# The gMLP gate of a two-layer decoder step: weights and biases prepared within the projection of v, v normalised by ScalarE in eight groups, one evacuation per block

## The reference, cut to what matters

```python
z = gelu(h @ w_in); u, v = split(z, 2)            # 3072 columns each
v = layer_norm(v, ln_g, ln_b)
ws = where(tril, w_s, 0)                          # 8 groups of 128x128
s = einsum('gts,bnsgc->bntgc', ws, vp) + b_s      # per chunk of 128 tokens, 384 columns per group
return (u * s) @ w_out, v                         # for the sample tokens v is an output too
```

## Time and profile before

| | |
|---|---|
| median of three runs | 2092.73 us (2079.18 to 2095.14) |
| profiled execution | 2092.21 us |
| its span, first to last instruction | 2090.40 us |
| TensorE matmul busy | 1862.7 us (89%) |
| VectorE busy | 1060.9 us (51%) |
| ScalarE busy | 540.6 us (26%) |
| GpSimd busy | 301.7 us (14%) |
| mean granted clock of TensorE | 0.933 |

### The profile page before, as it was taken

How to read it: one execution, slowest core, us unless ns; L and a number is a source line. 1 busy time by engine, 2 the same in 40 slices (tenths; PEclk the granted TensorE clock), 3 DMA queues, 4 the chain that set the end, 5 groups by cost and what they waited for, 6 DMA issues and landing times.

```text
span 2090.4 us, 35666 instructions
## 1 busy us (share of the span) xinstructions
PE 1862.7 (89%) x14217; PEld 1697.8 (81%) x14217; DVE 1060.9 (51%) x1400; ACT 540.6 (26%) x822; POOL 301.7 (14%) x263
## 2 busy tenths in 40 slices
PE   5866788687678879999999999969999999999998
PEld 4765555455455479999999999969999999999997
DVE  2599998987885345432333333274323353323321
ACT  4321232212222033321232233312313332212221
POOL 1220000000000001420241100022403223202300
PEclk8987898789899789999999999989999999999999
DMA  6247776899998722332323322211322323332321
GB/s 211 82 125 244 240 242 188 261 311 309 300 305 261 245 73 82 91 101 92 91 86 96 96 79 74 66 34 41 103 93 89 101 81 95 98 92 81 101 91 62
DMA packets 218302, 288.04 MB, mean 138 GB/s; under 512 B 12993, under 2 KB 149778, under 8 KB 217890
## 3 DMA queue, kind: packets, MB, share of 16 engines
q1 hardware_dynamic: 215306, 281.95, 42.3%
q0 software_dynamic: 656, 1.51, 0.5%
q10 hardware_dynamic: 2208, 2.75, 0.4%
HBM read 274.96 MB, written 11.21 MB: 137 GB/s over the span
## 4 chain that ended last, share of the span: by engine, by line
PE 70%; DVE 18%; SPq 3%; DMA 3%; issue 3%; ACT 2%; ACTq 0%; DVEq 0%
PE ps L1604 17%; PE ps L1606 17%; PE ps L1605 17%; PE ps L1425 4%; DVE kbuf L1109 4%; PE ps L1427 4%; PE ps L1426 4%; DVE Sc L1112 4%; DMA vbuf<-in_cache_v 2%; SPq L499 2%; SPq L498 1%; PE ps L1460 1%; DVE w_lo L488 1%; PE ps L1671 1%; PE ps L1393 1%
## 5 line engine op out<-in xcount | busy, mean ns | idle before, releaser
L488 DVE TENSOR_TENSOR w_lo<-raw,w_hi 128x1024 fp32r<-128x1024 f32 x238 | 328.0, 1386 | 486.9 <-ACT w_hi L481 485.6
L1604 PE MATMUL ps<-xg_hi,w_hi 128*128 128x260 f32 x1408 | 398.9, 283 | 0.5 <-DVE sTs L1380 0.5
L1606 PE MATMUL ps<-xg_hi,w_lo 128*128 128x260 f32 x1408 | 398.6, 283 | 0.0
L1605 PE MATMUL ps<-xg_lo,w_hi 128*128 128x260 f32 x1408 | 397.4, 282 | 0.0
L1425 PE MATMUL ps<-w_hi,xg_hi 128*128 128x256 f32 (+1 forms) x1200 | 366.1, 305 | 20.9 <-DVE w_lo L488 6.0
L481 ACT ACTIVATE w_hi<-raw 128x1024 fp32r<-128x1024 f32 x248 | 258.7, 1052 | 459.0 <-PE ps L1606 397.0
L1426 PE MATMUL ps<-w_lo,xg_hi 128*128 128x256 f32 (+1 forms) x1200 | 357.0, 297 | 0.0
L1427 PE MATMUL ps<-w_hi,xg_lo 128*128 128x256 f32 (+1 forms) x1200 | 355.8, 296 | 0.0
L1604 PE MATMUL ps<-h_hi,w_hi 128*128 128x260 f32 x1024 | 289.3, 282 | 0.0
L1606 PE MATMUL ps<-h_hi,w_lo 128*128 128x260 f32 x1024 | 289.1, 282 | 0.0
L1605 PE MATMUL ps<-h_lo,w_hi 128*128 128x260 f32 x1024 | 289.1, 282 | 0.0
(11 more groups left out here) (266 smaller groups left out, 2461.5 us busy)
## 6 DMA issues: line engine op xcount, KB each, us to landing
kbuf<-in_cache_k SPq DMA_DIRECT2D x256, 256.0 KB, 3.4
vbuf<-in_cache_v SPq DMA_DIRECT2D x256, 256.0 KB, 3.6
raw<-in_w_ffn_up SPq DMA_DIRECT2D x64, 512.0 KB, 3.8
raw<-in_w_ffn_down SPq DMA_DIRECT2D x64, 512.0 KB, 3.5
raw<-in_w_in_odd SPq DMA_DIRECT2D x48, 512.0 KB, 3.8
raw<-in_w_in_even SPq DMA_DIRECT2D x36, 512.0 KB, 5.0
raw<-in_w_out_odd SPq DMA_DIRECT2D x24, 512.0 KB, 3.6
raw<-in_w_out_even SPq DMA_DIRECT2D x12, 512.0 KB, 3.5
```

Source lines behind the costliest of these rows:

```text
L488: dve.tensor_tensor(w_lo[:, c.slot], raw[:, c.slot % 2], w_hi[:, c.slot].bitcast(F32), ALU.subtract).then_inc(lo_made, 1)
L1604: pe.matmul(out, wh, xh, start=kk == 0, stop=False, skip_group_check=True)
L1605: pe.matmul(out, wh, xl, start=False, stop=False, skip_group_check=True)
L1606: mm_ = pe.matmul(out, wl, xh, start=False, stop=kk == KC * groups - 1, skip_group_check=True)
```

## The change

- GpSimd issues the gate's DMAs (`gate_in`) after the first up projection of layer 0; the row ln_g keeps its old place. The first weights of the groups, `w00`, are loaded to all 128 partitions by two DMAs.
- The eight transposes follow the first block of v on TensorE, the ones matmul comes within the second block; the masks go into VectorE's first step and the copies to `RB` into ScalarE's, and the 24 bias rows, now one tile `tbs`, into VectorE's second step, which is unrolled too.
- After the statistics VectorE makes a bias of five columns, minus mean times reciprocal root (`lnb`); ScalarE normalises `vn` in eight groups of 384 columns, four activations each, and TensorE waits for its group alone. VectorE still normalises the samples.
- Per gated block VectorE has the evacuation only.
- The samples are transposed by TensorE ahead of block 20, where it waits for `vs_done`; VectorE scales them by `w00` and adds the bias after block 21.

```diff
@@ -299,12 +299,12 @@
         xg_lo = r("xg_lo", [P, KD, T], F32R)
         ones = r("ones", [P, P])
         vecs = r("vecs", [P, 81])
-        small = r("small", [P, 40])
+        small = r("small", [P, 48])
         GM, GF, LG, LB, SG = 0, 16, 32, 56, 80
         rstdN, ssN, rootN = small[:, 0:5], small[:, 5:10], small[:, 10:15]
         nlam, lamv = small[:, 15:16], small[:, 16:20]
         mvN = small[:, 20:30]
-        lnr = small[:, 30:35]
+        lnr, lnb = small[:, 30:35], small[:, -8:-3]
         shared = r.at
         rstdB = r("rstdB", [P, T])
         sq = r("sq", [P, 2, T])
@@ -385,9 +385,7 @@
         tmp2 = r("tmp2", [P, 2, T])
         bst5 = r("bst5", [P, 5, N_V, 6])
         sTs = r("sTs", [P, 24, NS])
-        tb = r("tb", [P, 2, P])
-        w00 = r("w00", [NS, 8])
-        dg = r("dg", [NS, 8, NS])
+        w00 = r("w00", [P, 8])
         body = r.at
         h_hi = r("h_hi", [P, 16, T], F32R)
         h_lo = r("h_lo", [P, 16, T], F32R)
@@ -400,6 +398,7 @@
         RB = r("RB", [P, 8, P])
         bsB = r("bsB", [P, 8, P])
         wsr = r("wsr", [P, 8, P])
+        tbs = r("tbs", [P, 24, P])
         r = Region(late)
         g_hi = r("g_hi", [P, 12, T], F32R)
         g_lo = r("g_lo", [P, 12, T], F32R)
@@ -462,6 +461,7 @@
                              "vs_done"))
         ein_ready, ein_read, lnrow_used, gate_loaded, lnb_loaded = (
             sem(n) for n in ("ein_ready", "ein_read", "lnrow_used", "gate_loaded", "lnb_loaded"))
+        lng_loaded, v_biased, tbs_made, s_ready = (sem(n) for n in ("lng_loaded", "v_biased", "tbs_made", "s_ready"))
         y_turned, y_copied, stored = sem("y_turned"), sem("y_copied"), sem("stored")
 
         SCALE = float(DH) ** -0.5
@@ -664,9 +664,23 @@
                     pool.tensor_tensor(tmp2[:, b, :], tmp1[:, b, :], tmp1[:, b, :], ALU.mult).then_inc(mid_made, 1)
                 return make
 
+            def gate_in():
+
+                pool.wait_ge(stored, 16)
+                pool.wait_ge(k_stored, 48)
+                for g in (0, 4):
+                    pool.dma_start(wsr[:, g:g + 4, :], w_s[0, g:g + 4].rearrange("g t s -> t g s")).then_inc(gate_loaded, 16)
+                pool.dma_start(bsB[:, :, :].rearrange("p g t -> p (g t)"),
+                               b_s[0].rearrange("g t -> (g t)").partition_broadcast(P)).then_inc(gate_loaded, 16)
+                for half in range(2):
+                    pool.dma_start(w00[64 * half:64 * half + 64, :], w_s[0][:, 0, 0].partition_broadcast(64),
+                                   allow_slow_non_contiguous=True).then_inc(gate_loaded, 16)
+
             def mlp(layer):
                 for h in range(2):
                     mids(f"up{layer}{h}", square(f"up{layer}{h}"), h_hi, h_lo)
+                    if layer == 0 and h == 0:
+                        gate_in()
 
             def gate(half):
                 name = f"u{half}"
@@ -688,15 +702,9 @@
             for n in range(KD):
                 add_square(2, n)
 
-            for g in (0, 4):
-                pool.dma_start(wsr[:, g:g + 4, :], w_s[0, g:g + 4].rearrange("g t s -> t g s")).then_inc(gate_loaded, 16)
-            pool.dma_start(bsB[:, :, :].rearrange("p g t -> p (g t)"),
-                           b_s[0].rearrange("g t -> (g t)").partition_broadcast(P)).then_inc(gate_loaded, 16)
-            pool.dma_start(w00[:, :], w_s[0][:, 0, 0].partition_broadcast(NS), allow_slow_non_contiguous=True
-                           ).then_inc(gate_loaded, 16)
-            pool.dma_start(lnrow[:, :], ln_v_g[0].partition_broadcast(NS)).then_inc(gate_loaded, 16)
+            pool.dma_start(lnrow[:, :], ln_v_g[0].partition_broadcast(NS)).then_inc(lng_loaded, 16)
             pool.wait_ge(vs_normed, 1)
-            pool.wait_ge(gate_loaded, 16 * 5)
+            pool.wait_ge(lng_loaded, 16)
             pool.tensor_tensor(vs[:, :], vs[:, :], lnrow[:, :], ALU.mult).then_inc(lnrow_used, 1)
             pool.wait_ge(lnrow_used, 1)
             pool.dma_start(lnrow[:, :], ln_v_b[0].partition_broadcast(NS)).then_inc(lnb_loaded, 16)
@@ -972,12 +980,19 @@
                         dst = vn[:, t, span(CW * mac, CW)] if t < NT else vs[:, span(CW * mac, CW)]
                         act.activation(dst, ps[rows, t, 0:CW], ACT.Gelu, scale=rstdN[rows, t:t + 1]).then_inc(nat_read, 1)
                     splits(c0, 4, i, 2 * mm + 1)
+                    if isinstance(i, int) and i == 0 and mm == 1:
+                        act.wait_ge(R_ready, 1)
+                        act.activation(RB[:, 0:4, :], ps[:, 7, :].rearrange("p (g t) -> p g t", g=4), ACT.Copy)
+                        act.activation(RB[:, 4:8, :], ps[:, 5, :].rearrange("p (g t) -> p g t", g=4), ACT.Copy).then_inc(R_copied, 1)
             repeat(act, macros // 2, v_step, first=1)
             act.wait_ge(v_var, 1)
             act.activation(lnr, mvN.rearrange("p (t c) -> p t c", c=2)[:, :, 1], ACT.Sqrt, bias=EPS).then_inc(v_root, 1)
-            act.wait_ge(R_ready, 1)
-            act.activation(RB[:, 0:4, :], ps[:, 7, :].rearrange("p (g t) -> p g t", g=4), ACT.Copy)
-            act.activation(RB[:, 4:8, :], ps[:, 0, :].rearrange("p (g t) -> p g t", g=4), ACT.Copy).then_inc(R_copied, 1)
+            act.wait_ge(v_biased, 1)
+            for g in range(8):
+                for t in range(NT):
+                    blk = vn[:, t, 3 * P * g:3 * P * (g + 1)]
+                    last = act.activation(blk, blk, ACT.Identity, scale=lnr[:, t:t + 1], bias=lnb[:, t:t + 1])
+                last.then_inc(v_normed, 1)
             act.wait_ge(vs_done, 1)
             act.dma_start(gv_sample[0].rearrange("s l e -> s (l e)"), vs[:, :]).then_inc(stored, 16)
             act.wait_ge(stored, 32)
@@ -1340,13 +1355,22 @@
                         out = bst5[rows, t].rearrange("p m c -> p (m c)")[:, span(6 * mac, 6)]
                         dve.bn_stats(out, src).then_inc(v_stats, 1)
                     splits(c0, 4, i, 2 * mm + 1)
-            repeat(dve, macros // 2, v_step, first=1)
-
-            dve.wait_ge(ws_turned, 1)
-            for g in range(2):
-                last = dve.tensor_tensor(wsT[:, 4 * g:4 * g + 4, :], ps[:, 5 + g, :].rearrange("p (g t) -> p g t", g=4),
-                                         C["causal"].unsqueeze(1).broadcast_to([P, 4, P]), ALU.mult)
-            last.then_inc(ws_masked, 1)
+                    if isinstance(i, int) and i == 0 and mm == 0:
+                        dve.wait_ge(ws_turned, 1)
+                        for g in range(2):
+                            last = dve.tensor_tensor(wsT[:, 4 * g:4 * g + 4, :], ps[:, 5 + g, :].rearrange("p (g t) -> p g t", g=4),
+                                                     C["causal"].unsqueeze(1).broadcast_to([P, 4, P]), ALU.mult)
+                        last.then_inc(ws_masked, 1)
+                    if isinstance(i, int) and i == 1:
+                        dve.wait_ge(R_copied, 1)
+                        for c in range(12 * mm, 12 * mm + 12):
+                            g = c // 3
+                            last = dve.scalar_tensor_tensor(tbs[:, c, :], RB[:, g, :], vecs[:, LB + c:LB + c + 1], bsB[:, g, :],
+                                                            ALU.mult, ALU.add)
+                        if mm == 1:
+                            last.then_inc(tbs_made, 1)
+            repeat(dve, macros // 2, v_step, first=2)
+
             dve.wait_ge(v_stats, 5 * N_V)
             for t in range(NT + 1):
                 rows = slice(0, P) if t < NT else slice(0, NS)
@@ -1354,32 +1378,31 @@
             last.then_inc(v_var, 1)
             dve.wait_ge(v_root, 1)
             chain(dve.reciprocal(lnr, lnr))
-            for t in range(NT):
-                dve.tensor_scalar(vn[:, t, :], vn[:, t, :], mvN[:, 2 * t:2 * t + 1], lnr[:, t:t + 1], ALU.subtract, ALU.mult
-                                  ).then_inc(v_normed, 1)
+            dve.scalar_tensor_tensor(lnb, mvN.rearrange("p (t c) -> p t c", c=2)[:, :, 0], -1.0, lnr, ALU.mult, ALU.mult
+                                     ).then_inc(v_biased, 1)
             dve.tensor_scalar(vs[:, :], vs[:, :], mvN[0:NS, 8:9], lnr[0:NS, 4:5], ALU.subtract, ALU.mult
                               ).then_inc(vs_normed, 1)
-            dve.wait_ge(gate_loaded, 16 * 5)
-            chain(dve.tensor_tensor(dg[:, :, :], ident[0:NS, 0:NS].unsqueeze(1).broadcast_to([NS, 8, NS]),
-                                    w00[:, :].unsqueeze(2).broadcast_to([NS, 8, NS]), ALU.mult))
-            dve.wait_ge(R_copied, 1)
+            dve.wait_ge(tbs_made, 1)
 
             def gate_block(c):
 
-                g = c // 3
-                chain(dve.scalar_tensor_tensor(tb[:, c % 2, :], RB[:, g, :], vecs[:, LB + c:LB + c + 1], bsB[:, g, :],
-                                               ALU.mult, ALU.add))
                 dve.wait_ge(ein_ready, c + 1)
                 blk = vn[:, :, P * c:P * c + P]
                 dve.scalar_tensor_tensor(blk, ps[:, 1 + c % 4, :].rearrange("p (t c) -> p t c", t=NT),
```

(52 more changed lines are left out.)

## The result

The kernel after the change took 2072.26 us, median of ten runs (2060.92 to 2079.68), against 2093.32 us of the kernel before (ten runs, 2079.18 to 2101.96): ratio 0.9904, 95% interval 0.988 to 0.9927. Timed again in the course of the experiments it had 0.9884 (0.9844 to 0.9924). The forecast was 2070 us.

What follows compares the result with a forecast made beforehand. TensorE is seven tenths of the chain of waits; the stretch looked at is the 58.2 us between v and u0. Starting u0 20.95 us earlier plus 2.15 us from its clock gives -23.1 us, 2070 on the median; range 2060 to 2080.

Steps and rivals of the forecast that it cites:

- Moved into v: In v: eight transposes and the ones matmul add 2.8 us of TensorE; masks, bias rows and copies cost nothing.
- GpSimd's DMAs: After the first up projection: moved gate DMAs take 6 to 8 us to issue within 98 us of cover, costing zero.
- To the first gate matmul: Last matmul of v to first gate matmul: first group normalised in 2.4 us, gate starts at 1378.2, or 1381.0 with v's 2.8.
- The gate: First gate matmul to u0: 4.6 + 18.6 + 2.1 + 1.4 = 26.7 us; u0 starts 20.95 us earlier.
- Samples and clock: Block 20 and u0: samples ready with 2.6 us slack; clock holds at u0, giving back 2.15 us.
- B: Rival, around the samples' transposes: the clock falls, +2.2 to +5.1 us, 2072 to 2075; chance 0.25.
- C: Rival, in the gate: TensorE does not set the pace; VectorE's 1.05 us a block adds 3.8 us, 2074; chance 0.12.
- D: Rival, at u0 or in v: weights not split or work stalls on a mask, losing 10 to 20 us; chance 0.06.
- E: Rival, in the gate: GpSimd's sample operations and the evacuations exclude each other, +25.5 us, 2095.5; chance 0.04.

## Why the prediction was right

- **Moved into v**, +2.8: measured +2.7 (177.25 against 174.54 with the work behind v). The masks, copies and bias rows cost nothing there, as forecast: a bias row took 0.345 us, no splits came late. Of the 8.8 us net that they cost behind v, 6 us are, by its rows, the collision with GpSimd that the prediction read off two rows of before.
- **GpSimd's DMAs**: zero, right; the size of the issuing was wrong by half, 15.2 us instead of 6 to 8. Three waits between issues (2.99, 5.90 and 2.67 us, put down to nothing that the profile shows) were not in the sum, though the timeline that holds had one such, 2.69 us. Why two more came, in front of the two 64-partition issues, was not tried.
- **To the first gate matmul**: 7.12 us against 6.9. The bias of five columns took 0.17, the group 2.6 instead of 2.4, because an activation with two columns takes 0.691 us rather than the 0.576 of the nearest row. The Trainium skill, "ScalarE: Activation LUTs", What ACT_TABLE_LOAD costs, would have given an estimated 0.69 us and 0.09 us of overlap; the trace agrees (0.691 us, 0.60 from one to the next).
- **The gate**: 26.5 against 26.7. Half clock 4.2 us instead of 4.6, a pace of 0.886 instead of 0.87, transposes 1.64 instead of 2.1, the end 1.03 instead of 1.4. The slower pace and the shorter ends partly cancel; that the sum is closer than its terms is luck.
- **Samples and clock**: slack 3.4 instead of 2.6; u0 at full clock, 2.3 us instead of 2.15.

Of the rivals, B did not happen, and the experiments give it its condition: 24 narrow transposes in 1.64 us lost the clock in none of the eleven profiled executions that have them, 96 did in the one. C did not happen either; its price for VectorE's pace was too high, 1.9 us at u0 (3.1 with the half clock that followed in that run) instead of 3.8, mainly since it left out that the transposes are hidden beside a VectorE that sets the pace. Normalising on VectorE, as the rule quoted in C would have it, cost 3.9 us with whole tiles and 13.0 with groups. D and E did not happen: the evacuations, one input of which is in PSUM, stayed at 0.75 us beside GpSimd.

That the ratio is 0.9904, on the near side of one per cent, while the stretches give 23 us, 1.1%, is within its interval; the chance was split about evenly there, for that reason.

## What to carry to other kernels

Time the stretch between two marks that the edit cannot touch: executions here differ by 17 us (1188 to 1205) ahead of the edited stretch, and the stretch itself repeated within 0.1 us (R 693.05 and 693.13 in two executions). Look at the clock at the marks too: v, which starts beside a stretch at half clock, repeated only within 0.64 us. Work that a hand-over does not depend on belongs beside a busy engine or into the idle time in front of the hand-over; here the second was free for TensorE and kept its clock at full. When two engines can do an operation, ask who else reads the same memory beside it and which of the two is needed next, not which is faster.

## What the runs showed of the hardware that was not expected

- GpSimd and VectorE held each other up in both directions. A VectorE operation that reads both inputs from SBUF, where the kernel's tiles lie, or normalises SBUF to SBUF, waited for GpSimd's operation to its end (bias rows of 3.26 and 6.64 us, groups of 5.05 and 7.98), and GpSimd in turn was longer behind VectorE's (an addition of 8.87 us instead of 6.7 behind the bias rows, a multiplication of 8.01 us beside a group of normalisations). Evacuations from PSUM went on at 0.75 us. The Trainium skill, "SBUF — State Buffer", SBUF: two separate sides, describes an exclusive lock held for a whole instruction; the traces agree.
- The granted clock fell to half 4.8 us into 96 transposes of 8x8 and stayed at full through 60 of 128x128 (6.6 us), both without idle time of TensorE.
